# Low halves ahead of level evictions, chunk products grouped by tile size, gated outputs behind the units, and the first inversion product between the units

## The reference

```
h = RMSNorm(x);  z = h @ W_in
o = concat[Retention(z_ret), RWKV7(z_rwkv), GLA(z_gla)]
x = x + o @ W_out
x = x + PEER(RMSNorm(x))
```

```
sa    = state @ (-kk_t)
state = state * w_t + sa (kk_t * a_t)^T + v_t k_t^T
o_t   = state @ r_t
```

## Time and profile before

| what | value |
|---|---|
| median of 3 runs | 2136.27 us (2130.84 to 2144.52) |
| the profiled execution's own time | 2131.4 us |
| its span, first to last instruction | 2129.6 us |
| TensorE busy | 2053.4 us (96%) |
| VectorE busy | 1421.4 us (67%) |
| ScalarE busy | 1332.3 us (63%) |
| GpSimd busy | 393.5 us (18%) |
| mean granted TensorE clock | 0.985 |

### The profile page before, as it was taken

How to read it: one execution, slowest core, us unless ns; L and a number is a source line. 1 busy time by engine, 2 the same in 40 slices (tenths; PEclk the granted TensorE clock), 3 DMA queues, 4 the chain that set the end, 5 groups by cost and what they waited for, 6 DMA issues and landing times.

```text
span 2129.6 us, 47165 instructions
## 1 busy us (share of the span) xinstructions
PE 2053.4 (96%) x15444; PEld 1861.0 (87%) x15444; DVE 1421.4 (67%) x3068; ACT 1332.3 (63%) x3144; POOL 393.5 (18%) x348
## 2 busy tenths in 40 slices
PE   8899999999999999999998999999999999999997
PEld 8788699999999888888797878999999998888885
DVE  6752469587888666666677534795888876666665
ACT  6531355799999555555565304558999995555554
POOL 0312036522222000000004020465222220000000
PEclk9998999999999999999999999999999999999998
DMA  6320444444444555555552105444444445555554
GB/s 234 101 79 2 158 157 166 171 158 158 160 164 167 179 197 189 188 195 197 179 193 99 61 22 180 156 158 158 167 168 159 158 158 195 188 191 196 197 191 174
DMA packets 47471, 338.95 MB, mean 159 GB/s; under 512 B 5648, under 2 KB 5776, under 8 KB 6928
## 3 DMA queue, kind: packets, MB, share of 16 engines
q1 hardware_dynamic: 47376, 337.73, 44.6%
HBM read 336.66 MB, written 1.05 MB: 159 GB/s over the span
## 4 chain that ended last, share of the span: by engine, by line
PE 84%; DVE 9%; ACT 3%; DMA 2%; issue 1%; POOL 0%; SPq 0%; DVEq 0%; ACTq 0%; PEldq 0%
PE ps L816 11%; PE ps L817 11%; PE ps L818 11%; PE ps L786 10%; PE ps L788 9%; PE ps L787 9%; PE ps L417 3%; PE ps L418 3%; PE ps L419 3%; PE ps L708 2%; PE ps L796 1%; PE ps L797 1%; DVE expert_lo L1365 1%; PE ps L433 1%; DVE expert_lo L1730 1%
## 5 line engine op out<-in xcount | busy, mean ns | idle before, releaser
L786 PE MATMUL ps<-h_t_hi,expert_hi 128*128 128x256 f32 x2048 | 592.1, 289 | 15.0 <-DVE expert_lo L1730 11.2
L787 PE MATMUL ps<-h_t_lo,expert_hi 128*128 128x256 f32 x2048 | 579.1, 283 | 0.0
L788 PE MATMUL ps<-h_t_hi,expert_lo 128*128 128x256 f32 x2048 | 578.9, 283 | 0.0
L1924 POOL TENSOR_TENSOR expert_lo<-w_ring,expert_hi 128x512 fp32r<-128x512 f32 x204 | 289.2, 1425 | 743.9 <-ACT expert_hi L1007 742.3
L786 PEld LDWEIGHTS ps<-h_t_hi,expert_hi 128*128 128x128 f32 x2048 | 392.3, 192 | 18.4 <-issue 8.3
L787 PEld LDWEIGHTS ps<-h_t_lo,expert_hi 128*128 128x128 f32 x2048 | 392.6, 192 | 0.0
L788 PEld LDWEIGHTS ps<-h_t_hi,expert_lo 128*128 128x128 f32 x2048 | 392.3, 192 | 0.0
L816 PE MATMUL ps<-expert_hi,act_hi 128*128 128x512 f32 x1008 | 392.1, 389 | 0.0
L817 PE MATMUL ps<-expert_lo,act_hi 128*128 128x512 f32 x1008 | 392.1, 389 | 0.0
L818 PE MATMUL ps<-expert_hi,act_lo 128*128 128x512 f32 x1008 | 392.1, 389 | 0.0
L1007 ACT CAST expert_hi<-w_ring 128x512 fp32r<-128x512 f32 x512 | 308.1, 614 | 102.4 <-PE ps L788 86.3
(11 more groups left out here) (306 smaller groups left out, 3192.0 us busy)
## 6 DMA issues: line engine op xcount, KB each, us to landing
w_ring<-u_t SPq DMA_DIRECT2D x128, 1024.0 KB, 4.8
w_ring<-v_t SPq DMA_DIRECT2D x128, 1024.0 KB, 4.8
w_ring<-w_in SPq DMA_DIRECT2D x32, 1024.0 KB, 4.9
w_ring<-w_q SPq DMA_DIRECT2D x16, 1024.0 KB, 4.8
w_ring<-w_out SPq DMA_DIRECT2D x8, 1024.0 KB, 4.8
big<-xconst SPq DMA_DIRECT2D x2, 1666.0 KB, 9.5
big<-keys SPq DMA_DIRECT2D x2, 1024.0 KB, 4.8
big<-rows SPq DMA_DIRECT2D x2, 576.0 KB, 11.4
```

Source lines behind the costliest of these rows:

```text
L786: pe.matmul(o, w_hi[:, c, :], HTH[:, d, :], start=d == 0, stop=False)
L787: pe.matmul(o, w_hi[:, c, :], HTL[:, d, :], start=False, stop=False)
L788: mm = pe.matmul(o, w_lo[:, c, :], HTH[:, d, :], start=False, stop=d == DC - 1)
L1924: pool.tensor_tensor(EL[:, m % 4, :], RING[:, m // 4, (m % 4) * 512:(m % 4 + 1) * 512], EH[:, m % 4, :].bitcast(F32), ALU.subtract).then_i ...
```

## The change

Four edits; the amount of arithmetic is the same.

1. On VectorE `w_lows(10)` moves ahead of the eviction `level(0)`, `w_lows(11)` ahead of `level(2)`, and `w_lows(12)` ahead of `decayed(1)`.
2. In `units` PE makes units 0 to 5, the 24 products of the inverse's start, units 6 to 9, the first product of step 0 for chunk 0 (`first_products(0, 0)`), units 10 and 11, and then the GLA outputs, now in PSUM banks 1 and 3 rather than 0 and 1. VectorE follows: `TI` after unit 5, `start_tt(0)` after unit 8, and the mask of the first product ahead of `start_tt(1)`.
3. `columns_turned` stands between the second products of step 0, and ACT's copies of it move from ahead of the squares to behind the two Silu.
4. For chunk 1 the products of one size stand together: the 6 of x with 128 rows run before the output products that cover the state, and then 6 state products for x, 6 state products for o, and the 6 and 6 others of o with u between them.

```diff
@@ units
-                for u in range(12):
-                    if u == 6:
-                        gla_outputs()
+                def unit(u):
...
+                for u in range(6):
+                    unit(u)
                 pe.wait_ge(proj_out, N_IN)
-                pe.wait_ge(gla_o_out, 2)
                 for u in range(12):
...
+                for u in range(6, 10):
+                    unit(u)
+                pe.wait_ge(ti_ready, 2)
+                first_products(0, 0)
+                for u in range(10, 12):
+                    unit(u)
+                gla_outputs()
@@ invert
                     for k in range(NT):
+                        if n == 0 and k == 0:
+                            continue
                         if n == 0:
-                            pe.wait_ge(ti_ready, 2)
-                            pe.wait_ge(unit_out, 6 * k + 6)
+                            pe.wait_ge(unit_out, 12)
...
-                    if n == 0:
-                        columns_turned()
                     for k in range(NT):
                         if n == 0:
                             pe.wait_ge(tt_ready, k + 1)
+                            pe.wait_ge(gla_o_out, k + 1)
+                            if k == 1:
+                                columns_turned()
@@ chunks, k = 1
+                x_part(1)
+                for f in range(2):
+                    out_product(1, 1, f)
+
+                pe.wait_ge(state_out, 1)
+                for h in range(NH):
+                    c, r = halves(h)
+                    mm = pe.matmul(PS[:, 4 * (h % 2), c * 64:(c + 1) * 64], AR[r, c, 1, 0, :], STATE[r, c, :], start=False, stop=True, skip_group_check=True)
+                mm.then_inc(chunk_x, 1)
+                pe.wait_ge(chunk_o_out, 1)
+                for h in range(NH):
+                    c, r = halves(h)
+                    pe.matmul(o_bank(h), AR[r, c, 1, 1, :], STATE[r, c, :], start=c == 0, stop=False, skip_group_check=True)
+                for h in range(NH):
+                    pe.matmul(o_bank(h), MASKED[:, NH + h, 3, :], VTOK[:, 1, h * 64:(h + 1) * 64], start=False, stop=False, skip_group_check=True)
+                u_part(1)
+                out_product(2, 1, 0)
+                pe.wait_ge(chunk_u_out, 2)
+                for h in range(NH):
+                    mm = pe.matmul(o_bank(h), MASKED[:, NH + h, 1, :], XU[:, 1, h * 64:(h + 1) * 64], start=False, stop=True, skip_group_check=True)
+                mm.then_inc(chunk_o, 1)
+                out_product(2, 1, 1)
+                for f in range(2):
+                    out_product(3, 1, f)
@@ scalar
-                for i in range(2):
-                    act.wait_ge(bk_done, i + 1)
-                    act.copy((BTOK, KTOK)[i], PS[:, 4 + i, 0:384]).then_inc(bk_out, 1)
...
                 act.activation(ZGLA[:, :, 384:768], ZGLA[:, :, 384:768], ACT.Silu).then_inc(silu_ready, 1)
+                for i in range(2):
+                    act.wait_ge(bk_done, i + 1)
+                    act.copy((BTOK, KTOK)[i], PS[:, 4 + i, 0:384]).then_inc(bk_out, 1)
@@ vector, the levels
                 w_lows(9)
+                w_lows(10)
                 dve.wait_ge(gacc_zero, 1)
                 level(0, 4)
-                w_lows(10)
                 rotate()
                 level(1, 4)
+                w_lows(11)
                 level(2, 4)
                 decayed(0, 6)
-                w_lows(11)
                 level(3, 6)
+                w_lows(12)
                 decayed(1, 4)
-                w_lows(12)
                 level(4, 6)
```

More of the change, by code:

```diff
@@ L531, in units, with first_products @@
                         mm.then_inc(mrow_done, 1)
+                for u in range(6, 10):
[5 more added lines that the diff above has]
+                gla_outputs()
+            tiles = [slice(0, 64), slice(64, 128)]
+            def first_products(n, k):
+                for h in range(NH):
+                    u = k * NH + h
+                    for r in tiles:
+                        mm = pe.matmul(PS[r, 2 * k, h * 64:(h + 1) * 64], MASKED[r, u, 0, r], TI[r, u, :], start=True, stop=True)
+                mm.then_inc(y_done, 1)
             def columns_turned():
@@ L622, in chunks @@
-                    mm.then_inc(chunk_o, 1)
-                    if k == 0:
-                        for h in range(NH):
-                            r = slice(64 * (h % 2), 64 * (h % 2) + 64)
-                            o, hc = PS[r, 3, (h // 2) * 64:(h // 2 + 1) * 64], slice(h * 64, (h + 1) * 64)
-                            pe.matmul(o, BTOK[:, hc], XU[:, 1, hc], start=True, stop=False)
-                            mm = pe.matmul(o, KTOK[:, hc], VTOK[:, 0, hc], start=False, stop=True)
-                        mm.then_inc(state_done, 1)
@@ L630, in chunks, with o_bank @@
-                    for f in range(2):
-                        out_product(2 * k + 1, 1, f)
+                def o_bank(h):
+                    return PS[:, 2 + 3 * (h % 2), h // 2 * 64:(h // 2 + 1) * 64]
+                x_part(0).then_inc(chunk_x, 1)
+                out_product(0, 1, 0)
+                u_part(0)
+                out_product(0, 1, 1)
+                pe.wait_ge(chunk_u_out, 1)
+                for h in range(NH):
+                    hc = slice(h * 64, (h + 1) * 64)
+                    pe.matmul(o_bank(h), MASKED[:, h, 1, :], XU[:, 1, hc], start=True, stop=False)
+                    mm = pe.matmul(o_bank(h), MASKED[:, h, 3, :], VTOK[:, 0, hc], start=False, stop=True)
@@ L1210, in _ @@
                     act.wait_ge(gla_o, t + 1)
[L1211 to L1214 removed]
+                    act.copy(HN[:, t, 640:1024], PS[:, 1 + 2 * t, 0:384]).then_inc(gla_o_out, 1)
                 act.wait_ge(ret_o_out, 1)
@@ L1485, in rwkv_units @@
                                       ALU.mult).then_inc(unit_out, 1)
-                    if u == 8:
-                        dve.wait_ge(eye_ready, 2)
-                        start_tt(0)
+                for u in range(6):
+                    unit(u)
                 ti_pairs = TI.rearrange("p (e r) n -> p r e n", r=2)
+                dve.wait_ge(eye_ready, 2)
                 for r in range(2):
@@ L1493, in rwkv_units @@
                                         PS[:, 2 * r, 0:384].rearrange("p (e n) -> p e n", e=NH)).then_inc(ti_ready, 1)
+                for u in range(6, 9):
+                    unit(u)
+                start_tt(0)
+                for u in range(9, 12):
+                    unit(u)
+                first_out(0, 0)
                 start_tt(1)
```

65 lines of the change are left out of this document (30 added, 35 removed).

## The result

The changed kernel took 2082.11 us (median of 4 runs, 2079.46 to 2083.76) against 2136.14 (4 runs, 2130.84 to 2144.52) for the kernel before: a ratio of 0.9742, 95% interval 0.9709 to 0.9776. Forecast were 2096.5 us and a range of 2083 to 2113. The direction was right and the gain larger than foretold: 54.0 us by the medians, where the sum had 39.7 and its best bounds 49.1. The time lies just under the range.

The account below looks back on a forecast made before the run. TensorE, busy 96% of the span, was taken as the bound, so only its waits and slow work in the mixers could go: 14.3 + 10.1 + 7.8 + 7.5 = 39.7 us. Forecast 2096.5 us, range 2083 to 2113.

Parts of the forecast that it names:

- the sum: Whole kernel: levels 14.3, units and step 0 10.1, chunks 7.8, first layer's chunk spell 7.5, together 39.7 us saved.
- best bounds: Most the sum could reach: 22.9 us for the levels and 4.3 a layer for the grouping, 49.1 in all, 2087 us.
- What bounds the kernel: TensorE busy 96% of the span; the change can only give back its waits or slow work in both layers' mixers.
- The levels: Both layers: low-part waits go, rotation wait becomes some 3.4 us, one slow spell a layer stays; 14.3 us saved.
- The change of port: Levels: moved low parts may contend with POOL for SBUF; no difference counted, at most 3 x 1.3 us a layer.
- The units and step 0: First unit to step 1's second products: no TensorE breaks, 17.84 us, despite thin covers; 10.1 us saved, 6.8 if spell stays.
- The chunks: x and o of chunk 1: grouping leaves two size changes, 5.8 us for 9.7; 3.9 a layer, 7.8 in all.
- the price of the clock: First layer's chunks: slow spell at mean clock 0.73, with TensorE busy throughout, counted as gone, 7.5 us saved.
- The spells only move: Rival: half-clock spells only move, so 7.5 and 3.3 us do not come; 28.9 us saved, 2107.4; chance 0.26.
- The levels gain nothing: Rival in the levels: DVE is the next bound and eviction waits replace low-part waits; 25.4 us saved, 2110.9; chance 0.11.
- The change of size isn't what costs: Rival in the chunks: a 64-row product takes 0.18 us anywhere, and the spell stays; 26.6 us saved, 2109.7; chance 0.06.
- A spell that lasts: Rival, units to end of chunks: clock stays low through unbroken small products, 33 us lost a layer, 2163; chance 0.04.

Follow-up runs that it names:

- full rows: Kernel before, in its own order, with chunk 1's state products over all 128 rows instead of 64, result not the reference's: 2109.36 us, ratio 0.9881.
- the second kernel on the rotation: Changed kernel with `turn_qk` behind level 2, level 1's eviction between the rotation's halves, and ScalarE's split of chunk 11 before its copies: 2076.06 us, ratio 0.9723.
- The 11 changes left in o: Changed kernel with the 64-row state products and 128-row products in o of chunk 1 back in turns, x still grouped: 2090.49 us, ratio 0.98.

## Why the prediction was right and where it fell short

**What bounds the kernel.** Right: dense products elsewhere, and in the mixers waits and a slow clock. 47.8 of the 51.9 us came from the three stretches that it named.

**The levels.** The mechanism held to a few tenths. The low parts run from 80.28 to 83.73 (foretold 80.1 to 83.7), no wait for low parts is left, and the rotation is late next with 3.57 us (foretold 3.4). Only in the second layer does another wait appear, 0.39 us for VectorE's decay of the scores. The size was 17.3 against 14.3. Two terms were too small. I left one spell at the lower clock in each layer, and the first layer has one and the second none (1.7 us). And the work at full rate is 23.1 and 23.3 us (24.77 less half of 3.4, and 23.34) where I worked out 24.6 and 24.1 from busy time and mean clock; what the 2.3 us between them were stays open. VectorE, whose work bounded the best case, is busy 23.03 and 23.87 us of the new stretches.

**The change of port.** The moved low parts of chunk 10 took 3.45 us in place of 4.11, between the two rates of the earlier trace rows; GpSimd worked for 2.2 us of them (80.36 to 82.58). The Trainium skill, page SBUF — State Buffer, section Who interferes with whom, has VectorE and GpSimd contend here; the three rates of one and the same instruction agree with it, and counting no difference was near enough.

**The units and step 0.** Right in the waits and the order. 17.46 and 17.47 us without any wait for 17.84 foretold, so even the thin covers (squares, square root) held. The second layer's spell went as said. What in edits 2 and 3 drives it off is not settled: the 2.58 us wait and the order of the small products go together in them, and no run parts the two.

**The chunks.** The prices were right: 0.21 us for a change against grouped products (0.19 taken from the sum of x and o; it is 0.14 against full rows), 0.06 a record for products of 64 rows side by side (0.05 taken), and for x and o of chunk 1 1.48 + 0.82 + 0.67 + 1.48 + 1.29 = 5.7 us in place of 9.66 (5.8 foretold).

**The step that failed is the price of the clock.** "The second layer, through the same turns of size, had it at 1.00. I count this spell as gone" put 7.5 us on the spell of one layer, cut at the edges of a window. The window of 30.48 us ended inside the spell, and that of 23.02 us just ahead of another, of 3.4 us, at 1264. By the steps of 2 us the chunks of before lost 12.0 us to the clock (7.5 in the sum), the levels 5.1 net of what is left (3.3 in the sum), the second layer's expert part 1.7 (none), and the units 4.1 (the same in the sum). The sum held 14.8 us of clock in all and the two profiles show 22.9: 8.1 of the 12.2 us that were missing between the profiled executions. Most of the rest is 1.2 in the levels, 0.8 in the units and 1.9 in the expert part, where TensorE's waits for one low part fell from 11.2 to 8.6 us in all. That fall is chance and not the change: the kernels with only edits 2 and 3 and with full rows have 8.5 and 8.6 us of it, and the second kernel on the rotation, with all four edits, has 11.1.

The medians add 2.1 us to that (54.0 for 51.9), for the same reason. The 37 runs of before on three chips have mean clocks from 0.973 to 0.985, 0.980 on average; the profiled execution, with 0.985, is as high as the best of them. I set that execution against the median as a whole (4.9 us) and did not ask what made it faster. Over all runs, by time multiplied by clock, the change gave 25.8 us at the full clock, where the sum without its clock terms has 24.9, and 30.2 us of clock (42.7 to 12.5), where the sum has 14.8. So by the runs waits and prices were foretold within 1 us in all (by the two profiles within 4), and the clock was put at half its size.

Had I priced a whole spell in both layers' chunks, as the runs with edit 1 alone and without edit 4 show it (20.5 us or more at the lower level, so 10.2 for each where the sum had 7.5 for one), the sum would have been 13 us larger, and the forecast of 2083.5 us within 2 us of the result. That is said with hindsight; the trace of before shows one such spell, and only the later runs show the second.

**The rivals.** *The spells only move* (0.26) is refuted for the long spells by the three single edits; were it true of all, 14.8 us of the sum would be missing and not the 10.8 that I took off. I had set beside it the Trainium skill, page TensorE: Matmul & The Clock Gate, Why this matters for your kernels, which ties the slow level to idle gaps between bursts. The measurement decides against that reading for the chunks: the spells begin after 13 us without idle time, stay through 20 us without any, and go when products of one size stand together. *The levels gain nothing* fell with 17.3 us. *The change of size isn't what costs* fell with 0.82 and 0.67 us for the twelve records of 64 rows side by side, 0.06 each where it had 0.18, and with the full-rows kernel. *A spell that lasts* did not come: in the 29.10 us and 29.19 us of the chunks the clock is 1.00.

## What to carry to other kernels

Price the granted clock over the whole span in small steps and not over the windows of the argument, for the slow spells are long and begin and end outside them; and look at the clock of several runs before taking a profile's good layer for the rule. Small products of different row counts that took turns cost 0.21 us a change more than grouped ones, and mostly more again in clock, so group them by size. Full rows gained as much, but here with another result than the reference's; operands filled up with zeros were not tried. When a wait for an elementwise engine goes, look at what is queued behind the instruction that it waited for next: here the waits of 3.57 us behind the rotation fell to 1.34 only when the eviction behind it and the ScalarE copies moved too, and to 2.84 without that.

## What the runs showed of the hardware that I had not expected

- The clock falls in work without idle time. Four kernels keep all turns of 64 and 128 rows in both layers (before, edit 1 alone, edits 2 and 3 alone, the change without edit 4), and each of their eight chunk stretches spends time at 1.2 GHz: seven of them 13.6 to 23.9 us, the second layer of before 3.4. The 11 changes left in o brought 3.3 and 3.4 us; grouped sizes and full rows brought none. Why the turns do it is not shown.
- A product that does less can take longer. A 64-row pair between 128-row pairs takes 0.36 us, a full 128-row pair there 0.22, and 64-row products side by side 0.11 to 0.14 a pair (0.67 and 0.82 us for twelve records).
- The same kernel's runs lie up to 24 us apart, and mostly by the clock: for before 2126.13 us at a mean clock of 0.985 and 2149.67 at 0.975, and time multiplied by clock is 2094 and 2096. Over its 37 runs that product lies between 2089 and 2101. The changed kernel's runs lie within 4.3 us in one series and 12 in the other (0.991 to 0.995).
